# A norm's squares added up on VectorE instead of TensorE, at five sums of a joined two-block kernel

## What is computed

```
def rms_norm(x, g):
    xf = x.astype(jnp.float32)
    var = jnp.mean(xf * xf, axis=-1, keepdims=True)
    return (xf * lax.rsqrt(var + EPS)).astype(x.dtype) * g
```

## Time and profile before

| | us |
|---|---|
| median of 3 runs (2355.15 to 2359.11) | 2357.45 |
| the profiled execution, its own time | 2356.58 |
| its span, first to last instruction | 2354.9 |
| PE (TensorE matmul) busy | 2177.0 (92%) |
| DVE (VectorE) busy | 1459.5 (62%) |
| ACT (ScalarE) busy | 782.6 (33%) |
| POOL (GpSimd) busy | 285.3 (12%) |
| mean granted TensorE clock | 0.963 |

### The profile page before, as it was taken

How to read it: one execution, slowest core, us unless ns; L and a number is a source line. 1 busy time by engine, 2 the same in 40 slices (tenths; PEclk the granted TensorE clock), 3 DMA queues, 4 the chain that set the end, 5 groups by cost and what they waited for, 6 DMA issues and landing times.

```text
span 2354.9 us, 26875 instructions
## 1 busy us (share of the span) xinstructions
PE 2177.0 (92%) x10667; PEld 1741.9 (74%) x10667; DVE 1459.5 (62%) x2256; ACT 782.6 (33%) x1161; POOL 285.3 (12%) x196
## 2 busy tenths in 40 slices
PE   6998878888999999799999999999999798999998
PEld 4876666566888886687888888887877577687876
DVE  5623778637848583477777777777777632443342
ACT  4362222334324333423333332233222233332232
POOL 0012666414224030000000000000000000000000
PEclk9998899998999999899999999999999799999998
DMA  4331111323434343111111111111111022023320
GB/s 139 99 89 37 45 38 53 90 88 109 126 110 132 115 129 87 45 54 45 46 46 48 51 45 47 52 45 46 45 47 53 18 89 81 28 85 85 87 82 37
DMA packets 311132, 164.54 MB, mean 70 GB/s; under 512 B 6268, under 2 KB 307938, under 8 KB 311010
## 3 DMA queue, kind: packets, MB, share of 16 engines
q1 hardware_dynamic: 311010, 162.85, 23.8%
HBM read 160.73 MB, written 2.10 MB: 69 GB/s over the span
## 4 chain that ended last, share of the span: by engine, by line
PE 72%; DVE 19%; issue 5%; ACT 3%; POOL 0%; SPq 0%; DMA 0%; DVEq 0%; ACTq 0%; POOLq 0%
PE bank L474 16%; PE bank L476 16%; PE bank L475 16%; DVE KC L1710 3%; DVE MT L1732 3%; DVE QC L1712 3%; DVE QQ L1717 2%; PE bank L819 2%; PE bank L509 2%; PE bank L493 1%; PE bank L491 1%; PE bank L492 1%; PE bank L885 1%; PE bank L798 1%; DVE PP L1725 1%
## 5 line engine op out<-in xcount | busy, mean ns | idle before, releaser
L1344 DVE TENSOR_TENSOR wl<-stage,wh 128x1024 fp32r<-128x1024 f32 (+1 forms) x248 | 311.7, 1258 | 661.9 <-ACT wh L947 661.8
L474 PE MATMUL bank<-hh,wh 128*128 128x512 f32 x1408 | 586.3, 416 | 30.6 <-DVE hl L1365 14.7
L947 ACT ACTIVATE wh<-stage 128x1024 fp32r<-128x1024 f32 (+1 forms) x248 | 260.1, 1050 | 964.3 <-PE bank L476 610.0
L476 PE MATMUL bank<-hh,wl 128*128 128x512 f32 x1408 | 554.4, 394 | 0.0
L475 PE MATMUL bank<-hl,wh 128*128 128x512 f32 x1408 | 553.1, 393 | 0.0
L474 PEld LDWEIGHTS bank<-hh,wh 128*128 128x128 f32 x1408 | 267.2, 190 | 97.2 <-issue 36.8
L476 PEld LDWEIGHTS bank<-hh,wl 128*128 128x128 f32 x1408 | 266.9, 190 | 58.9
L475 PEld LDWEIGHTS bank<-hl,wh 128*128 128x128 f32 x1408 | 268.3, 191 | 52.9 <-issue 4.3
L474 PE MATMUL bank<-gh,wh 128*128 128x512 f32 x432 | 179.4, 415 | 16.0 <-DVE gl L1573 6.6
L428 POOL TENSOR_TENSOR mprod<-stage,gs 128x1024 f32<-128x1024 f32 x64 | 130.8, 2044 | 465.6 <-DMA stage<-in_ada_w 460.7
L476 PE MATMUL bank<-gh,wl 128*128 128x512 f32 x432 | 170.6, 395 | 0.0
(11 more groups left out here) (305 smaller groups left out, 3188.3 us busy)
## 6 DMA issues: line engine op xcount, KB each, us to landing
stage<-in_hg_w_in SPq DMA_DIRECT2D x80, 512.0 KB, 3.6
stage<-in_ada_w SPq DMA_DIRECT2D x48, 512.0 KB, 3.6
stage<-in_w_up SPq DMA_DIRECT2D x44, 512.0 KB, 3.8
stage<-in_ft_w_in SPq DMA_DIRECT2D x32, 512.0 KB, 3.9
stage<-in_w_in SPq DMA_DIRECT2D x28, 512.0 KB, 3.8
stage<-in_w_down SPq DMA_DIRECT2D x16, 512.0 KB, 3.7
stage<-in_hg_w_out SPq DMA_DIRECT2D x16, 512.0 KB, 3.6
stage<-in_ft_w_out SPq DMA_DIRECT2D x16, 512.0 KB, 3.5
```

The lines of the kernel that those rows point to most:

```text
L474: pe.matmul(bank[t % NLIN][:], wh[:, s, k, :], xh[:, k, :], start=a, stop=False)
L476: mm = pe.matmul(bank[t % NLIN][:], wl[:, s, k, :], xh[:, k, :], start=False, stop=b)
L947: do(A.activation(wh[:, l % NSPLIT, 0:nk, :], stage[:, u["slot"], 0:nk, :], ACT.Copy), "hi_ready")
L1344: do(X.tensor_tensor(wl[:, l % NSPLIT, 0:nk, :], stage[:, u["slot"], 0:nk, :], wh[:, l % NSPLIT, 0:nk, :].bitcast(F32), ALU.subtract), f"s ...
```

## The change

ScalarE still squares every tile. VectorE now adds the squares of the first seven tiles, tile n into the buffer of tile n, as they come: `running(m, n)` for n = 1 to 6 makes `sq[n % 2] += sq[(n - 1) % 2]`. TensorE then makes two products with the ones matrix at the end of the stage: part 0 is the sum of tiles 0 to 6, part 1 the square of tile 7. A square of tile n >= 2 waits for the addition that read its buffer, no longer for a matmul. In m = 3 the second, scaled, square goes to two buffers of `facc` and has an addition of its own.

The order of VectorE around it: in m = 1, 3, 5 and 6 the addition of tile n-1 stands between `weights_behind` of tile n and `residual` of tile n. In m = 2 the addition of tile j-1 is the last instruction of pair j, behind `gl`.

```diff
+            def sum_of(m, part, width=T, b=3, buf=sq):
+                if part == 0:
+                    pe.wait_ge(S("sq_add"), SQ_ADDS[m] + (12 if m == 3 else 6))
+                else:
+                    pe.wait_ge(S("sq_ready"), KT * m + (2 * KT if m == 3 else KT))
+                pe.matmul(bank[b][:, 0:width], ones[:], buf[:, part, 0:width], start=(part == 0), stop=(part == 1)
+                          ).then_inc(S("sq_used"), 1)
...
             for n in range(1, KT):
                 units_to(T_OUT + n)
-                sum_mm(KT + n - 1, n - 1)
-            sum_mm(2 * KT - 1, KT - 1)
+            for part in range(2):
+                sum_of(1, part)
...
+            def square_of(m, n, src, name, value, width=T):
+                if n < 2:
+                    act.wait_ge(S("sq_used"), SQ_SUMS[m])
+                else:
+                    act.wait_ge(S("sq_add"), SQ_ADDS[m] + (2 if m == 3 else 1) * (n - 1))
+                act.wait_ge(S(name), value)
+                do(A.activation(sq[:, n % 2, 0:width], src, ACT.Square), "sq_ready")
+                if m == 3:
+                    if n == 0:
+                        act.wait_ge(S("flo"), FT)
+                    do(A.activation(facc[:, n % 2, :], src, ACT.Square, scale=vcol("final1", n)), "sq_ready")
...
+            def running(m, n, width=T):
+                if not 0 < n < KT - 1:
+                    return
+                dve.wait_ge(S("sq_ready"), KT * m + (2 * n + 2 if m == 3 else n + 1))
+                if n > 1:
+                    dve.wait_ge(S("sq_add"), SQ_ADDS[m] + (2 if m == 3 else 1) * (n - 1))
+                do(X.tensor_tensor(sq[:, n % 2, 0:width], sq[:, n % 2, 0:width], sq[:, (n - 1) % 2, 0:width], ALU.add), "sq_add")
+                if m == 3:
+                    do(X.tensor_tensor(facc[:, n % 2, :], facc[:, n % 2, :], facc[:, (n - 1) % 2, :], ALU.add), "sq_add")
...
             for n in range(KT):
                 weights_behind(T_OUT + n)
+                running(1, n - 1)
                 residual(T_OUT + n, n)
...
                     p += 1
+                    if r == 1:
+                        running(2, j - 1, CT)
                 for n in range(KT):
                     weights_behind(t1_ + n)
+                    if r == 2:
+                        running(3, n - 1)
                     residual(t1_ + n, n)
```

More of the change, by code:

```diff
@@ L63, in modulation_sums @@
     return 2 * i if i < 2 * KT else i + 2 * KT
+SQ_ADDS = {1: 0, 2: 6, 3: 12, 5: 24, 6: 30}
+SQ_SUMS = {1: 8, 2: 10, 3: 12, 5: 16, 6: 18}
 def host_constants():
@@ L742, in _ @@
                         mm.then_inc(S("cx_T"), 1)
-                        if j:
-                            sum_mm(2 * KT + j - 1, j - 1, CT)
                 if r < 2:
@@ L747, in _ @@
                     if r == 1:
-                        sum_mm(3 * KT - 1, KT - 1, CT)
+                        for part in range(2):
+                            sum_of(2, part, CT)
                     units_to(t1_ + KT - 1)
@@ L752, in _ @@
                         units_to(t1_ + n, ("flo", pairs) if n == 0 else None)
-                        for k in ([n - 1] if n else []) + ([n] if n == KT - 1 else []):
-                            sum_mm(3 * KT + 2 * k, k)
-                            sum_mm(3 * KT + 2 * k + 1, k, b=4)
+                    for part in range(2):
+                        sum_of(3, part)
+                        sum_of(3, part, b=4, buf=facc)
                 pairs += len(ROUND[r])
@@ L868, in _ @@
                 if n:
-                    sum_mm(5 * KT + n - 1, n - 1)
                     turn_x(n - 1)
-            sum_mm(6 * KT - 1, KT - 1)
+            for part in range(2):
+                sum_of(5, part)
             turn_x(KT - 1)
@@ L917, in _ @@
                     else:
-                        residual_units(t + 4, lambda k: sum_mm(6 * KT + k, k), mixed_in)
+                        units_to(t + 4, mixed_in)
+                        units_to(t + 4 + KT - 1)
+                        for part in range(2):
+                            sum_of(6, part)
             assert pos[0] == len(units)
@@ L982, in split_high, with residual_tiles @@
                         do(A.activation(dst[:, k, :], hf[:, k % 2, 0:width], ACT.Copy), "hh_ready")
-            def residual_tiles(t0, j0):
+            def residual_tiles(t0, m):
                 for n in range(KT):
                     finish_tile(t0 + n)
-                    square(j0 + n, xT[:, n, :], evac_name(t0 + n), (t0 + n) // NLIN + 1)
+                    square_of(m, n, xT[:, n, :], evac_name(t0 + n), (t0 + n) // NLIN + 1)
             def col_roots(i, eps_scale, between):
@@ L1139, in _ @@
                 do(A.activation(gh[:, h, :], oT[:, h, :], ACT.Copy), "oa_hi")
-            residual_tiles(T_OUT, KT)
-            root(rs, bank[3], value=2 * KT)
+            residual_tiles(T_OUT, 1)
+            root(rs, bank[3], value=SQ_SUMS[2])
             split_high(1, hh)
@@ L1164, in _ @@
                         do(A.activation(craw[:, j, :], bank[4 + j % 2][:, 0:CT], ACT.Copy), "cx_ev")
-                        square(2 * KT + j, craw[:, j, :], "cx_ev", j + 1, CT)
+                        square_of(2, j, craw[:, j, :], "cx_ev", j + 1, CT)
                 for n in range(KT):
@@ L1168, in _ @@
                     if r == 1 and n == 0:
-                        root(rs, bank[3], CT, value=3 * KT)
+                        root(rs, bank[3], CT, value=SQ_SUMS[3])
                     if r == 1:
@@ L1174, in _ @@
                         done = (evac_name(t1_ + n), (t1_ + n) // NLIN + 1)
-                        square(3 * KT + 2 * n, xT[:, n, :], *done)
-                        square(3 * KT + 2 * n + 1, xT[:, n, :], *done, scale=vcol("final1", n))
-            root(rs, bank[3], value=5 * KT)
+                        square_of(3, n, xT[:, n, :], *done)
+            root(rs, bank[3], value=SQ_SUMS[5])
             root(rs2, rs2, ready="x1_square", value=1)
@@ L1272, in _ @@
                 finish_tile(T_HO + n)
-                square(5 * KT + n, xT[:, n, :], evac_name(T_HO + n), (T_HO + n) // NLIN + 1)
+                square_of(5, n, xT[:, n, :], evac_name(T_HO + n), (T_HO + n) // NLIN + 1)
                 if n:
                     place_x(n - 1)
-            root(rs, bank[3], value=6 * KT)
+            root(rs, bank[3], value=SQ_SUMS[6])
             place_x(KT - 1)
@@ L1318, in _ @@
                         finish_tile(t + 4 + n)
-            residual_tiles(len(tiles) - KT, 6 * KT)
-            root(rs, bank[3], value=7 * KT)
+            residual_tiles(len(tiles) - KT, 6)
+            root(rs, bank[3], value=SQ_SUMS[6] + 2)
             for i in range(2 * TT):
@@ L1791, in _ @@
                 weights_behind(T_HO + n)
+                running(5, n - 1)
                 residual(T_HO + n, n, gate(0))
@@ L1846, in _ @@
                         weights_behind(t + 4 + n)
+                        if gi > 4:
+                            running(6, n - 1)
                         residual(t + 4 + n, n, gate(1))
```

## The result

The changed kernel takes 2340.55 us (median of 4 runs, 2338.73 to 2342.94) where the kernel before, on the same chip, takes 2358.28 (4 runs): ratio 0.9926, 95% interval 0.9908 to 0.9943. That is 17.7 us less. The forecast was 2345.2 us, 12.25 less, with a range of 2336 to 2350; so sign and range held. The profiled execution took 2338.9 us.

What follows compares the result with a forecast made beforehand. TensorE sets the pace in m = 1, 3, 5, 6; in m = 2 an equally long VectorE and ScalarE loop runs beside it. Terms -4.35 + 5.3 - 3.3 - 4.6 - 5.3 = -12.25 gave 2345.2 us, range 2336 to 2350.

Steps and rivals of the forecast that it cites:

- signs of being wrong: Wrong if m = 2's loop keeps to 12.1, m = 3 runs at 4.1 us per unit, or an addition takes much over 0.61.
- rival 3: In m = 2, GpSimd's operation blocks the additions on five pairs, at most 4.5 us: 2349.7 us; chance 0.06.
- the last `gl` later by 2.65: End of m = 2: five pairs slip 3.8 us, 1.15 is swallowed, so the last `gl` comes 2.65 us later.
- the half clock 2.2: Behind m = 2, in `w_down`'s first unit: TensorE restarts at 1.2 GHz after a long pause, costing 2.2 us.
- the end swallowed 1.15 us: Last pair of m = 2: the second `wl` waited for TensorE before, so 1.15 us of the delay is absorbed.
- The slip: m = 2: the square waits for the addition behind `gl`, moving the VectorE and ScalarE loop by 0.76 us per pair.
- Rival 1: m = 2's loop has unseen slack, so it saves 2.6 us instead of costing 5.3: 2337.3 us; chance 0.20.
- a loop at 12.9: Sign of the forecast in m = 2: VectorE's loop takes 12.9 us.
- a pause of 5 us or more: Sign in m = 2: TensorE pauses 5 us or more ahead of the last block of `w_down`'s first unit.
- -5.5, not -10.3: m = 3: the last `wh` comes 5.5 us earlier, though the matmuls leaving the path total 10.3 us.
- Rival 2: Every removed matmul counts, m = 3 too (-10.3 + 2.2), together with rival 1: 2332.5 us; chance 0.05.
- Rival 4: Half clock behind the new pause in round two's `w_down` lasts through seven further units: 2381 us; chance 0.04.

Runs made afterwards that it cites:

- m = 2 alone: The kernel before with the change made at m = 2 only; 2361.11 us, ratio 1.0015.
- the filled kernel: The changed kernel with unread matmuls in TensorE's pauses, ten in round two and four in round three; 2341.52 us, ratio 0.9931.
- m = 2 undone: The changed kernel with the sum of m = 2 put back on TensorE; 2342.96 us, ratio 0.9931.
- the kernel with the additions in the gaps: The changed kernel with additions moved into VectorE's waits, ahead of `wl` in m = 1, 3, 5 and ahead of `gl` in m = 2; 2325.77 us.
- m = 3 undone: The changed kernel with the two sums of m = 3 put back on TensorE; 2346.65 us, ratio 0.9964.
- m = 2's addition in the gap: The changed kernel with only m = 2's addition moved, ahead of `gl` into VectorE's wait for `gh`; 2337.16 us, ratio 0.9911.
- the fastest one with its fillers: The kernel with all additions moved into waits, plus four unread matmuls in round three's 2.24 us pause; 2326.98 us, ratio 0.9864.

## Why the prediction was right, and where it was not

**m = 1: -4.35 forecast, -3.5 and -3.7 measured.** The tail was right: +0.95 forecast, 6.78 - 5.82 = 0.96 measured, with the half clock in both matmuls. The six matmuls were not all gained, since GpSimd slowed two rounds down to 6.5 and 6.6 us. One of the prediction's own signs of being wrong came true here: two additions took 1.78 us, much over 0.61. The contention of rival 3 exists; it struck in m = 1, where I had not looked. The additions of m = 2 took 0.42 us each, and began 0.7 us behind the end of GpSimd's operation. By the Trainium skill, "SBUF — State Buffer", section "Who interferes with whom", a VectorE instruction with two SBUF inputs and a GpSimd instruction that reads SBUF shut each other out; the trace agrees (1.78 against 0.68 us, and GpSimd's L438 2.16 against 1.26).

**m = 2: +5.3 forecast, +3.5 and +3.6 measured.** This is the step that failed in size. Its three terms: the last `gl` later by 2.65 was forecast, 0.62 measured (1.44 with m = 2 alone, 1.69 in the filled kernel); the second matmul 0.43, measured 0.41; the half clock 2.2, measured 2.4 and 2.0. The loop of VectorE and ScalarE was the limit, as argued, and the end swallowed 1.15 us, as forecast. The slip itself came: the square waited 0.82 us, and from `gl` to the next `wl` it is 2.46 us instead of 1.73, +0.73 where 0.76 was forecast. What was wrong is to make five of them 3.8 us of loop, read from one pair (12.10). The kernel before takes 12.49, 12.10, 12.24, 11.96 and 9.53 us for the five, the changed kernel 12.68 or 12.69 four times and 10.26: 60.99 - 58.32 = 2.7 us. One pair before had 0.28 of the slip already (2.01 instead of 1.73), and from there to `gl` the five were 0.7 us longer before (10.76 and 10.36 in two of them, where the changed kernel has 10.22). There VectorE's operations beside GpSimd took longer; how much shows in two pairs of the kernel before, with GpSimd's product and without it:

```profile
756.83 3.06 DVE L1608 SCALAR_TENSOR_TENSOR facc<-fraw,V,facc 128x512 f32<-128x512 f32 x2
756.98 2.37 POOL L428 TENSOR_TENSOR mprod<-stage,gs 128x1024 f32<-128x1024 f32 x1 [7.02 <-DMA stage<-in_ada_w]
...
768.78 1.54 DVE L1608 SCALAR_TENSOR_TENSOR facc<-fraw,V,facc 128x512 f32<-128x512 f32 x2
```

From a pair's first `wl` to its `gl` it is 9.46 to 10.76 us with GpSimd and 7.80 without, in both kernels. So it is GpSimd's work beside it that makes this loop as long as TensorE's pace; that is read from the pairs, and no run here takes the work away. Besides, the changed kernel enters the five pairs 0.9 us earlier. So does the one with m = 2 undone, so that is not the additions' doing; the filled kernel doesn't, and that is why its last `gl` is late. These 0.9 and the 1.1 between 3.8 and 2.7 are the 2.0 by which the last `gl` was forecast too late. Nearly all of the 0.9 lies in the pair before: 9.46 and 9.31 us from `wl` to `gl` in the changed kernel and with m = 2 undone, 10.22 in the kernel before and 10.23 in the filled one. GpSimd's operations fell elsewhere in it (the first one began 1.5 us after the start of VectorE's last convolution steps in the changed kernel, 0.2 us after it in the kernel before); why they did is open. One reading of the prediction was wrong without harm: ScalarE's second copy of a pair did wait for TensorE before (0.19 to 1.00 us), but VectorE's second subtraction did not wait for that copy. Rival 1, no slip at all, is refuted by m = 2 alone. The signs "a loop at 12.9" and "a pause of 5 us or more" came out as 12.7 and 4.4.

**m = 3: -3.3 forecast, -2.7 measured twice.** The step "-5.5, not -10.3" measured -5.58: VectorE's and ScalarE's round is what is late next. The tail measured +2.9 against +2.2, since the clock stayed at half into the last of the sums' matmuls; with m = 2 undone it rose sooner and the tail is 2.05. That the round is set by the addition's place between `wl` and the residual, not by its 0.68 us, is shown by the kernel with the additions in the gaps: there the last copy comes 10.1 us earlier, behind the 1.6 of the clock. Rival 2's -10.3 was thus to be had by another order.

**m = 5: -4.6 forecast, -4.3 measured; m = 6: -5.3, -5.4.** In m = 5 the six matmuls gave 5.16 us instead of 5.3, and part 1 was covered but for 0.16 us.

**Where the errors went.** m = 1 was 0.8 too good, m = 2 1.8 too bad, m = 3 0.6 and m = 5 0.3 too good: they cancel, and that -12.5 stands beside -12.25 is luck. The first profile's gain, 17.7 us like that of the medians, holds 5.2 us of untouched stages, and the second profile has 2.2 us there with the other sign. So the 5.5 us by which the medians beat the forecast aren't shown to be the change's. The edited kernels have such a gap as well: the stages of the five norms and the medians give -18.4 and -14.4 us for m = 2 undone, -9.8 and -10.7 for m = 3 undone, -18.7 and -22.1 for m = 2's addition in the gap, -15.7 and -17.8 for the pauses filled, -31.2 and -31.6 for the additions in the gaps. Rival 4 did not come: behind the pause of 4.4 us the half clock lasted some 5 us.

## What to carry to other kernels

When work moves to an engine with time to spare, its place in that engine's list counts for more than its length: the same 36 additions gave 12.5 us in the five stages with each behind the operation that others wait for, and 31.2 us with 30 of them moved into waits that the engine had anyway (0.7% and 1.3% of the time by the medians; 1.6 us of the second is a clock that did not fall). A loop that two engines close between them is read over all its rounds, not one, since its rounds differ by 0.5 us here. And a difference of some 5 us between two kernels should be read stage by stage at like instructions, with a second profile of each, before any of it is called the change's.

## What the runs showed that I had not expected

- Untouched code moves. At the copy of 461.22, ahead of every edit, the difference from the kernel before is -1.5 in the changed kernel and +6.7 in the fastest one with its fillers. 2 of these 8 us are there at the copy of 192.39, and 6 arise behind it, where TensorE, VectorE and GpSimd take turns in short pieces; the granted clock from 280 to 310 us was 0.85 in the one and 0.77 in the other.
- A pause of 2.24 us behind the same instructions was followed by half clock in five kernels and by full clock in three others that left it unfilled; the three kernels with a second profile did the same in it. What in the order decides it is open. It is worth 1.6 us.
- At the end of round two a pause of 1.3 us was followed by clock 1.00 in both kernels that had it unfilled, one of 4.4 to 5.2 us by 0.50 in all five profiles that had it: 2.0 to 2.4 us beyond the pause itself. Matmuls that nobody reads take that back in the stage, but not, in 5 runs, in the kernel's time.
